# Experts in rounds of two chunks: both gates and ups, two down pieces, then both chunks' transposes

## The chip, the cores and the metric

The program runs on one NeuronCore of one Trainium2 chip. The metric is the device time of one execution in microseconds, lower is better. TensorE does the matrix products, VectorE and ScalarE the elementwise work and the reading of PSUM, GpSimd a few squares in the norms, and SyncE issues nearly all DMAs.

## The reference

A decoder trunk of two layers for 256 tokens of width 1024, float32. Layer 0 is a recurrent block and a dense SwiGLU, layer 1 is attention in a window and a mixture of eight experts. The change touches only the experts:

```python
logits = (h @ w_router)                       # 256 x 8
top_vals, top_idx = lax.top_k(logits, 2)
comb = one_hot(top_idx) weighted by softmax(top_vals)
for e in range(8):
    out += comb[:, e] * ((silu(h @ w_gate[e]) * (h @ w_up[e])) @ w_down[e])
```

`w_gate[e]` and `w_up[e]` are 1024 x 3584 and `w_down[e]` is 3584 x 1024.

## The kernel before

**Tiling.** An expert's 3584 hidden columns are cut into 14 chunks (`NCH`) of 256. A chunk has three pieces of weights of 1 MB each: gate, up and down. That makes 42 pieces (`PIECES`) per expert and 336 for eight. Each expert has room for 96 tokens (`CAP`); tokens beyond that would go to extra tiles in a loop behind the experts, which does not run with these inputs.

**Precision.** TensorE multiplies operands of the type fp32r, and each operand is split in two, a high part (the value cast, by ScalarE) and a low part (value minus high part, by VectorE). A product is three passes: high x high, low x high, high x low (`PASSES`). So a piece goes through four hands. SyncE loads it into one of 14 slots of a ring. ScalarE casts it into `w_hi` (line 656). VectorE subtracts it into `w_lo` (line 1237). TensorE uses both. `w_hi` and `w_lo` have room for three pieces (`PARTS`), so the cast of piece n waits until TensorE is through with piece n - 3 (`parts_used`). A slot of the ring is free again when its low part is done (`lo_done`), and SyncE's next load waits for that (lines 418 to 424).

**A chunk on TensorE.** `gate_up` (line 1807) makes gate and up of the chunk's 96 tokens, 24 matmuls of 256 columns each, in one PSUM bank, even and odd chunks in different banks. ScalarE applies silu (line 669), VectorE multiplies with up (line 1249). `turn_h` (line 1814) transposes the product in two transposes. ScalarE and VectorE evict it as high and low part (lines 673 and 1253, called `stage_ht`). `down` (line 1829) multiplies with the down piece, 12 matmuls of 512 columns, and adds up over all 14 chunks in two banks.

**Order.** Every engine runs a list written out by hand, without a planner. In `body`, for each chunk c from 2 to 13, TensorE does gate and up of c, down of c - 2, then the turn of c - 1. The down piece lags two chunks. `lead` starts the first expert with gate and up of chunks 0 and 1 and the turn of chunk 0. `cross` joins two experts: the next expert's chunks 0 and 1 stand between the last two downs of this one. `finish` ends the last expert. The tables `LEAD`, `BODY`, `CROSS` and `LAST` give the order of the pieces, which is the order of loads and of splits.

**Work strewn in.** Between the chunks stand these. `gather` picks the next expert's tokens with 32 matmuls (line 1795) and `stage_xg` evicts them. `weights_back` transposes the gate weights (line 1767) and ScalarE copies them (line 660). `stage_y` copies an expert's result out of PSUM, half by ScalarE (line 677) and half by VectorE (line 1258), once its last down is through. `scatter` multiplies it back to the tokens (line 1777) and `add_back` adds it to h on VectorE (line 1231). `next_onehots` makes the next expert's selection (lines 1262 and 1264). During expert 0 VectorE also builds the tables of overflow in pieces (`weights_of_choice`, `overflow_hits`, `overflow_tiles`, `overflow_columns`, `overflow_list`, lines 1173 to 1222). In the last expert's `finish`, `turn_back` transposes h in 16 transposes (line 1868) ahead of the last two downs.

## Time and profile before

| | |
|---|---|
| Three runs | 1494.76, 1498.63, 1498.02 us; median 1498.02 |
| The profiled execution's own time | 1499.07 us |
| Its span, first to last instruction | 1497.2 us |
| Mean granted clock of TensorE | 0.987 of full |
| Busy: TensorE matmuls, weight loads | 1459.7 us (97%), 1331.3 us (89%) |
| Busy: VectorE, ScalarE, GpSimd | 1161.0 us (78%), 919.4 us (61%), 42.7 us (3%) |
| DMA | 426.14 MB, mean 285 GB/s |
| The experts | from about 478 us to about 1482 us |

TensorE (PE) appears twice: PE are the matmuls and PEld the loads of the stationary operand, which overlap them. Matmuls are pipelined and the ends of their rows are modelled, so the distance from one start to the next says more than a duration. DVE is VectorE, ACT is ScalarE, SPq is the queue of DMAs that SyncE issues. A line number is that of the kernel shown above.

### The profile page before, as it was taken

What the parts mean: (1) busy time and instruction counts of PE and PEld (TensorE: products, weight loads), DVE (VectorE), ACT (ScalarE), POOL (GpSimd) and SP (SyncE); (2) the same over time, 40 slices, a digit from 0 to 9 for tenths busy, and PEclk for the clock granted to TensorE, in tenths of its full rate; (3) what the DMA queues carried; (4) which work ended last, traced back from release to release, by engine and by line L of the source; (5) the groups of instructions that cost most, each with busy time, mean ns of one, the idle gap of its engine ahead of it and who ended that gap; (6) DMA issues with size and microseconds to landing.
All of it is one profiled execution on the core that took longest, in us unless ns stands there. A gap on an engine that the chain in (4) does not pass through costs nothing.

```text
span 1497.2 us, 25391 instructions
## 1 busy us (share of the span) xinstructions
PE 1459.7 (97%) x10682; PEld 1331.3 (89%) x10682; DVE 1161.0 (78%) x1094; ACT 919.4 (61%) x904; POOL 42.7 (3%) x62
## 2 busy tenths in 40 slices
PE   8999999998899999999999999999999999999996
PEld 7889999998888999889889988988988898898894
DVE  6666555557545998898889888888888988888895
ACT  3744434343433776676767676676676766767675
POOL 2020000003001000000000000000000000000000
PEclk9999999999997999999999999999999999999999
DMA  8456555554206999999999899999989988999940
GB/s 325 141 205 211 184 182 197 175 192 141 85 29 279 383 381 351 359 355 342 342 353 383 333 350 352 346 340 362 360 319 363 375 334 340 366 342 341 362 174 30
DMA packets 60000, 426.14 MB, mean 285 GB/s; under 512 B 7024, under 2 KB 7152, under 8 KB 8688
## 3 DMA queue, kind: packets, MB, share of 16 engines
q1 hardware_dynamic: 58752, 422.60, 75.5%
q10 hardware_dynamic: 1136, 1.91, 0.4%
q8 instruction: 86, 1.41, 0.4%
q14 instruction: 26, 0.21, 0.0%
HBM read 423.44 MB, written 1.05 MB: 284 GB/s over the span
## 4 chain that ended last, share of the span: by engine, by line
PE 94%; DVE 3%; ACT 1%; POOL 1%; issue 1%; DMA 0%; DVEq 0%; ACTq 0%; SPq 0%; POOLq 0%
PE ps L1807 41%; PE ps L1829 21%; PE ps L1507 11%; PE ps L1529 5%; PE ps L1429 2%; PE ps L1795 2%; PE ps L1569 2%; PE ps L1777 2%; PE ps L1672 1%; PE ps L1814 1%; DVE w_lo L823 1%; PE ps L1461 1%; PE ps L1616 1%; PE ps L1444 1%; POOL hn L1387 1%
## 5 line engine op out<-in xcount | busy, mean ns | idle before, releaser
L1237 DVE TENSOR_TENSOR w_lo<-ring,w_hi 128x2048 fp32r<-128x2048 f32 x336 | 763.8, 2289 | 101.9 <-ACT w_hi L656 100.3
L656 ACT CAST w_hi<-ring 128x2048 fp32r<-128x2048 f32 x336 | 640.1, 1910 | 143.0 <-PE ps L1807 143.0
L1807 PE MATMUL ps<-w_hi,xg_hi 128*96 128x256 f32 x1792 | 249.3, 281 | 1.2 <-DVE xg_lo L1243 1.2
L1807 PE MATMUL ps<-w_lo,xg_hi 128*96 128x256 f32 x1792 | 242.1, 277 | 0.0
L1807 PE MATMUL ps<-w_hi,xg_lo 128*96 128x256 f32 x1792 | 241.6, 277 | 0.0
L1807 PEld LDWEIGHTS ps<-w_lo,xg_hi 128*96 128x96 f32 x1792 | 215.4, 161 | 1.2 <-DVE w_lo L1237 1.2
L1807 PEld LDWEIGHTS ps<-w_hi,xg_lo 128*96 128x96 f32 x1792 | 215.8, 161 | 0.0
L1807 PEld LDWEIGHTS ps<-w_hi,xg_hi 128*96 128x96 f32 x1792 | 213.6, 161 | 1.3 <-DVE xg_lo L1243 1.3
L823 DVE TENSOR_TENSOR w_lo<-ring,w_hi 128x2048 fp32r<-128x2048 f32 x56 | 129.8, 2320 | 80.9 <-ACT w_hi L471 80.9
L471 ACT CAST w_hi<-ring 128x2048 fp32r<-128x2048 f32 x56 | 106.5, 1903 | 112.1 <-PE ps L1507 94.1
L1829 PE MATMUL ps<-w_lo,ht_hi 128*96 128x512 f32 x448 | 123.4, 397 | 0.2 <-DVE w_lo L1237 0.2
L1829 PE MATMUL ps<-w_hi,ht_hi 128*96 128x512 f32 x448 | 122.9, 396 | 0.3 <-ACT w_hi L656 0.3
L1829 PE MATMUL ps<-w_hi,ht_lo 128*96 128x512 f32 x448 | 122.2, 394 | 0.0
L673 ACT CAST ht_hi<-ps 128x192 fp32r<-128x192 f32 x112 | 35.6, 318 | 117.9 <-PE ps L1814 117.7
L1829 PEld LDWEIGHTS ps<-w_lo,ht_hi 128*96 128x96 f32 x448 | 71.6, 161 | 33.6 <-DVE w_lo L1237 2.2
L1829 PEld LDWEIGHTS ps<-w_hi,ht_lo 128*96 128x96 f32 x448 | 72.2, 161 | 31.9
L1829 PEld LDWEIGHTS ps<-w_hi,ht_hi 128*96 128x96 f32 x448 | 67.1, 162 | 16.0 <-ACT w_hi L656 0.5
L1507 PE MATMUL ps<-u_hi,w_hi 128*128 128x256 f32 x448 | 58.1, 282 | 0.7 <-ACT u_hi L503 0.7
L1507 PE MATMUL ps<-u_hi,w_lo 128*128 128x256 f32 x448 | 57.3, 281 | 0.0
L1507 PE MATMUL ps<-u_lo,w_hi 128*128 128x256 f32 x448 | 57.3, 281 | 0.0
L1507 PEld LDWEIGHTS ps<-u_hi,w_hi 128*128 128x128 f32 x448 | 54.9, 189 | 1.6 <-ACT u_hi L503 1.1
L1253 DVE TENSOR_TENSOR ht_lo<-ps,ht_hi 128x192 fp32r<-128x192 f32 x112 | 38.9, 347 | 21.9 <-ACT ht_hi L673 21.9
(275 smaller groups left out, 1379.5 us busy)
## 6 DMA issues: line engine op xcount, KB each, us to landing
ring<-in_moe_w_gate SPq DMA_DIRECT2D x112, 1024.0 KB, 6.4
ring<-in_moe_w_up SPq DMA_DIRECT2D x112, 1024.0 KB, 6.2
ring<-in_moe_w_down SPq DMA_DIRECT2D x112, 1024.0 KB, 6.3
ring<-in_ffn_w_gate SPq DMA_DIRECT2D x14, 1024.0 KB, 4.8
ring<-in_ffn_w_up SPq DMA_DIRECT2D x14, 1024.0 KB, 4.8
ring<-in_ffn_w_down SPq DMA_DIRECT2D x14, 1024.0 KB, 4.8
ring<-in_lru_w_in SPq DMA_DIRECT2D x7, 1024.0 KB, 12.1
ring<-in_attn_w_qkv SPq DMA_DIRECT2D x6, 1024.0 KB, 4.8
```

What stands on the lines that cost most here:

```text
L471: nc.scalar.copy(w_hi[:, j % PARTS], ring[:, slot_at(j)]).then_inc(hi_done, 1)
L656: nc.scalar.copy(w_hi[:, (SPLITS + n) % PARTS], ring[:, s]).then_inc(hi_done, 1)
L673: nc.scalar.copy(ht_hi[:, c % 2], ps[:, 6 + c % 2, 0:2 * CAP].rearrange("p (f n) -> p f n", f=2)).then_inc(ht_hi_ready, 1)
L823: V.tensor_tensor(w_lo[:, j % PARTS], ring[:, slot_at(j)], w_hi[:, j % PARTS].bitcast(F32), ALU.subtract).then_inc(lo_done, 1)
L1237: V.tensor_tensor(w_lo[:, part], ring[:, ORDER_MOE[n % SLOTS]], w_hi[:, part].bitcast(F32), ALU.subtract).then_inc(lo_done, 1)
L1253: V.tensor_tensor(ht_lo[:, c % 2], ps[:, 6 + c % 2, 0:2 * CAP].rearrange("p (f n) -> p f n", f=2), ht_hi[:, c % 2].bitcast(F32), ALU.subtr ...
L1429: mm = nc.tensor.matmul(ps[:, p % 4, f * T:(f + 1) * T], col[:, k, f * P:(f + 1) * P], u_raw[:, k], start=(k == 0), stop=(k == KC - 1))
L1507: mm = nc.tensor.matmul(ps[:, 2 * (c % 2) + f, m * T:(m + 1) * T], w[b][:, k, f * P:(f + 1) * P], us[a][:, k], start=(k == 0 and (a, b) == ...
L1529: mm = nc.tensor.matmul(ps[:, 4 + d // 2, (d % 2) * T:(d % 2 + 1) * T], w[b][:, f, d * P:(d + 1) * P], fs[a][:, c % 2, f], start=False, st ...
L1569: mm = nc.tensor.matmul(ps[:, a % 2, b * T:(b + 1) * T], us[m][:, k, b * P:(b + 1) * P], w[n][:, k], start=False, stop=(k == KC - 1 and n ...
L1807: mm = nc.tensor.matmul(ps[0:CAP, c % 2, m * CHF:(m + 1) * CHF], xs[a][:, k], w[b][:, k], start=(k == 0 and (a, b) == (0, 0)), stop=(k == ...
L1829: mm = nc.tensor.matmul(ps[0:CAP, 2 + g, :], hs[a][:, c % 2, f], w[b][:, f, g * 512:(g + 1) * 512], start=(c == 0 and f == 0 and (a, b) == ...
```

## The change

The loop over chunks goes in steps of two. TensorE does gate and up of c and of c + 1, then the downs of c - 2 and c - 1, then the turns of c and c + 1. Loads, splits and evictions follow that order on SyncE, ScalarE and VectorE. `lead` turns chunk 1 as well, since the first body no longer does. In `cross` the two chunks of the next expert come first, then both last downs, then the transposes of the gate weights and the turns of the next expert's chunks 0 and 1. Scatters stand behind the turns of rounds c = 4 and 6, add-backs at the end of rounds 6 and 8, the copy of the gate weights behind `stage_y`. The numbers of instructions of each kind stay as they are.

```diff
         LEAD = [(m, c, 0) for c in range(2) for m in ("gate", "up")]
-        BODY = [(m, c - 2 * (m == "down"), 0) for c in range(2, NCH) for m in ("gate", "up", "down")]
-        CROSS = [("gate", 0, 1), ("up", 0, 1), ("down", NCH - 2, 0), ("gate", 1, 1), ("up", 1, 1), ("down", NCH - 1, 0)]
+        BODY = [(m, c, 0) for r in range(2, NCH, 2)
+                for m, c in (("gate", r), ("up", r), ("gate", r + 1), ("up", r + 1), ("down", r - 2), ("down", r - 1))]
+        CROSS = [("gate", 0, 1), ("up", 0, 1), ("gate", 1, 1), ("up", 1, 1), ("down", NCH - 2, 0), ("down", NCH - 1, 0)]
...
# ScalarE
             def body(i, y_at):
-                for c in range(2, NCH):
+                for c in range(2, NCH, 2):
                     n = BODY_AT + 3 * (c - 2)
+                    if c > 2 or y_at is not None:
+                        silu(i, c - 1, n - 3)
                     split(i, n)
+                    split(i, n + 1)
+                    if c == 2 and y_at is None:
+                        silu(i, 1, 3)
                     if c == 2 and y_at is not None:
                         stage_y(i, y_at)
-                    split(i, n + 1)
-                    silu(i, c - 1, n - 2 if c > 2 else y_at - 1 if y_at is not None else 3)
+                        weights_back(i - 1)
+                    split(i, n + 2)
                     stage_ht(i, c - 2)
-                    split(i, n + 2)
+                    stage_ht(i, c - 1)
+                    split(i, n + 3)
+                    silu(i, c, n + 1)
+                    split(i, n + 4)
+                    split(i, n + 5)
 
             def cross(i):
+                silu(i, NCH - 1, END_AT - 3)
+                stage_xg(i + 1)
                 split(i, END_AT)
-                act.wait_ge(parts_used, PIECES * i + (SPLITS + END_AT - 2 + 1))
-                stage_xg(i + 1)
                 split(i, END_AT + 1)
-                silu(i, NCH - 1, END_AT - 2)
+                split(i, END_AT + 2)
                 stage_ht(i, NCH - 2)
-                split(i, END_AT + 2)
+                stage_ht(i, NCH - 1)
                 split(i, END_AT + 3)
+                silu(i + 1, 0, END_AT + 1 - PIECES)
                 split(i, END_AT + 4)
-                weights_back(i)
-                silu(i + 1, 0, END_AT + 1 - PIECES)
+                split(i, END_AT + 5)
+
+            def finish(i, first=False):
+                silu(i, NCH - 1, END_AT - 3)
+                split(i, END_AT)
+                split(i, END_AT + 1)
+                stage_ht(i, NCH - 2)
                 stage_ht(i, NCH - 1)
...
# VectorE: body
-                for c in range(2, NCH):
+                for c in range(2, NCH, 2):
                     n = BODY_AT + 3 * (c - 2)
+                    if c > 2 or y_at is not None:
+                        gate_times_up(i, c - 1)
                     split(i, n)
+                    split(i, n + 1)
+                    if c == 2 and y_at is None:
+                        gate_times_up(i, 1)
                     if c == 2 and y_at is not None:
                         stage_y(i, y_at)
-                    split(i, n + 1)
-                    gate_times_up(i, c - 1)
+                    split(i, n + 2)
                     stage_ht(i, c - 2)
-                    split(i, n + 2)
-                    if first and c == 3:
+                    stage_ht(i, c - 1)
+                    split(i, n + 3)
+                    gate_times_up(i, c)
+                    split(i, n + 4)
+                    if first and c == 4:
                         weights_of_choice()
+                    if first and c == 6:
+                        overflow_tiles()
+                    if first and c == 8:
+                        overflow_columns(1)
+                    split(i, n + 5)
                     if first and c == 4:
                         overflow_hits()
-                    if first and c == 5:
-                        overflow_tiles()
-                    if first and c in (6, 7):
-                        overflow_columns(c - 6)
-                    if first and c == 9:
+                    if first and c == 6:
+                        overflow_columns(0)
+                    if first and c == 10:
                         overflow_list()
-                    if back and c in (4, 6):
-                        add_back(i - 1, c - 4)
-                        add_back(i - 1, c - 3)
+                    if back and c in (6, 8):
+                        add_back(i - 1, c - 6)
+                        add_back(i - 1, c - 5)
                     if c == 8:
                         next_onehots(i)
...
# TensorE
                 gate_up(i, 0, 0)
                 gate_up(i, 1, 2)
                 turn_h(i, 0)
+                turn_h(i, 1)
 
             def body(i, to_come, back=True, first=False):
-                for c in range(2, NCH):
+                for c in range(2, NCH, 2):
                     n = BODY_AT + 3 * (c - 2)
                     gate_up(i, c, n)
-                    down(i, c - 2, n + 2, first)
-                    if back and c in (3, 5):
-                        scatter(i - 1, c - 3)
-                        scatter(i - 1, c - 2)
-                    if c == 11 and to_come:
+                    gate_up(i, c + 1, n + 2)
+                    down(i, c - 2, n + 4, first)
+                    down(i, c - 1, n + 5)
+                    if c == 10 and to_come:
                         if back:
                             pe.wait_ge(added, 4 * i)
                         gather(i + 1)
-                    turn_h(i, c - 1)
+                    turn_h(i, c)
+                    turn_h(i, c + 1)
+                    if back and c in (4, 6):
+                        scatter(i - 1, c - 4)
+                        scatter(i - 1, c - 3)
 
             def cross(i):
                 pe.wait_ge(xg_ready, 2 * i + 4)
                 gate_up(i, 0, END_AT)
+                gate_up(i, 1, END_AT + 2)
+                down(i, NCH - 2, END_AT + 4)
+                down(i, NCH - 1, END_AT + 5)
                 weights_back(i)
-                down(i, NCH - 2, END_AT + 2)
-                turn_h(i, NCH - 1)
-                gate_up(i, 1, END_AT + 3)
-                down(i, NCH - 1, END_AT + 5)
                 turn_h(i + 1, 0)
+                turn_h(i + 1, 1)
...
             def finish(i, q, first=False):
-                turn_h(i, NCH - 1)
                 if first:
                     turn_back()
                 down(i, NCH - 2, END_AT)
```

## Rows read from the trace of the kernel before

**Rows 1.** The page's chain that ended last: shares of the span by engine.

```profile
PE 94%; DVE 3%; ACT 1%; POOL 1%; issue 1%; DMA 0%; DVEq 0%; ACTq 0%; SPq 0%; POOLq 0%
```

**Rows 2.** Groups by line, 480 to 1440 us: busy us, mean ns; idle before, releaser.

```profile
L1237 DVE TENSOR_TENSOR w_lo<-ring,w_hi 128x2048 fp32r<-128x2048 f32 x323 | 734.0, 2289 | 96.8 <-ACT w_hi L656 95.2
L656 ACT CAST w_hi<-ring 128x2048 fp32r<-128x2048 f32 x323 | 615.4, 1910 | 138.6 <-PE ps L1807 138.6
...
L1231 DVE TENSOR_TENSOR h<-ps,h 128x512 f32<-128x512 f32 x28 | 17.9, 683 | 0.0
```

**Rows 3.** Waits, 480 to 1440 us: who waited for whom, us, times, longest.

```profile
ACT w_hi L656 <- PE ps L1807: 138.6, 184, 1.1
...
PEld ps L1829 <- DVE w_lo L1237: 1.5, 7, 0.2
PEld ps L1807 <- DVE w_lo L1237: 1.2, 7, 0.2
...
SPq L424 <- DVE w_lo L1237: 548.6, 212, 6.0
```

**Rows 4.** Timeline of a steady chunk: start us, us, engine, line, operation, count.

```profile
711.61 0.33 PE L1814 MATMUL ps<-cst,hn 96*128 96x96 f32 x2
711.72 1.14 PE L1807 MATMUL ps<-w_hi,xg_hi 128*96 128x256 f32 x8
...
712.70 1.07 PE L1807 MATMUL ps<-w_hi,xg_lo 128*96 128x256 f32 x8
...
717.24 1.09 PE L1829 MATMUL ps<-w_hi,ht_hi 128*96 128x512 f32 x4
...
720.04 0.33 PE L1814 MATMUL ps<-cst,hn 96*128 96x96 f32 x2
```

**Rows 5.** Timeline behind an expert's border.

```profile
728.79 1.16 PE L1807 MATMUL ps<-w_hi,xg_hi 128*96 128x256 f32 x8
...
734.45 1.09 PE L1829 MATMUL ps<-w_hi,ht_hi 128*96 128x512 f32 x4
...
737.44 0.58 ACT L677 COPY hn<-ps 96x512 f32<-96x512 f32 x1 [3.63 <-PE ps L1829]
...
742.20 0.94 PEld L1807 LDWEIGHTS ps<-w_lo,xg_hi 128*96 128x96 f32 x8 [0.18 <-DVE w_lo L1237]
...
754.60 1.89 PE L1777 MATMUL ps<-gt_mem,hn 96*128 96x256 f32 x8
...
756.44 1.17 PE L1807 MATMUL ps<-w_hi,xg_hi 128*96 128x256 f32 x8
...
762.12 1.09 PE L1829 MATMUL ps<-w_hi,ht_hi 128*96 128x512 f32 x4
```

**Rows 6.** Timeline of the last transposes and the last two down pieces.

```profile
1472.88 0.49 PE L1814 MATMUL ps<-cst,hn 96*128 96x96 f32 x4
...
1473.22 1.91 PE L1868 MATMUL ps<-cst,h 128*128 128x128 f32 x16
...
1475.42 1.17 PE L1829 MATMUL ps<-w_hi,ht_hi 128*96 128x512 f32 x4 [0.30 <-ACT w_hi L656]
...
1476.44 1.10 PE L1829 MATMUL ps<-w_hi,ht_lo 128*96 128x512 f32 x4
...
1477.75 1.18 PE L1829 MATMUL ps<-w_lo,ht_hi 128*96 128x512 f32 x4 [0.21 <-DVE w_lo L1237]
```

**Rows 7.** Timeline at the end of expert 0's lead.

```profile
487.49 4.50 DVE L1237 TENSOR_TENSOR w_lo<-ring,w_hi 128x2048 fp32r<-128x2048 f32 x2 [0.86 <-ACT w_hi L656]
...
489.11 1.16 PE L1807 MATMUL ps<-w_hi,xg_hi 128*96 128x256 f32 x8
...
491.90 0.42 DVE L1249 TENSOR_TENSOR hn<-ps,hn 96x256 f32<-96x256 f32 x1
```

**Rows 8.** Timeline of TensorE in the attention.

```profile
406.55 0.63 PE L1595 MATMUL ps<-cst,ring 128*128 128x128 f32 x4 [3.09 <-DVE ring L1075]
```

**Rows 9.** Windows: busy us of each engine, PEclk, DMA share, GB/s.

```profile
408.00:411.30 3.30, 3.30 (x10) 2.44 (x10) 1.45 (x3) 1.50 (x8) 0.00 (x0) 0.50 0.57 241
```

More of the change, by code:

```diff
@@ L696, in body @@
             def body(i, y_at):
-                for c in range(2, NCH):
+                for c in range(2, NCH, 2):
                     n = BODY_AT + 3 * (c - 2)
+                    if c > 2 or y_at is not None:
+                        silu(i, c - 1, n - 3)
                     split(i, n)
+                    split(i, n + 1)
+                    if c == 2 and y_at is None:
+                        silu(i, 1, 3)
                     if c == 2 and y_at is not None:
                         stage_y(i, y_at)
-                    split(i, n + 1)
-                    silu(i, c - 1, n - 2 if c > 2 else y_at - 1 if y_at is not None else 3)
+                        weights_back(i - 1)
+                    split(i, n + 2)
                     stage_ht(i, c - 2)
-                    split(i, n + 2)
+                    stage_ht(i, c - 1)
[3 more added lines that the diff above has]
+                    split(i, n + 5)
             def cross(i):
+                silu(i, NCH - 1, END_AT - 3)
+                stage_xg(i + 1)
                 split(i, END_AT)
-                act.wait_ge(parts_used, PIECES * i + (SPLITS + END_AT - 2 + 1))
-                stage_xg(i + 1)
                 split(i, END_AT + 1)
-                silu(i, NCH - 1, END_AT - 2)
+                split(i, END_AT + 2)
                 stage_ht(i, NCH - 2)
-                split(i, END_AT + 2)
+                stage_ht(i, NCH - 1)
                 split(i, END_AT + 3)
+                silu(i + 1, 0, END_AT + 1 - PIECES)
                 split(i, END_AT + 4)
-                weights_back(i)
-                silu(i + 1, 0, END_AT + 1 - PIECES)
-                stage_ht(i, NCH - 1)
                 split(i, END_AT + 5)
             def finish(i, first=False):
-                silu(i, NCH - 1, END_AT - 2)
+                silu(i, NCH - 1, END_AT - 3)
+                split(i, END_AT)
+                split(i, END_AT + 1)
                 stage_ht(i, NCH - 2)
-                split(i, END_AT)
                 stage_ht(i, NCH - 1)
-                split(i, END_AT + 1)
                 if first:
@@ L1311, in cross @@
             def cross(i):
+                gate_times_up(i, NCH - 1)
+                stage_xg(i + 1)
                 split(i, END_AT)
-                stage_xg(i + 1)
                 split(i, END_AT + 1)
-                gate_times_up(i, NCH - 1)
+                split(i, END_AT + 2)
                 stage_ht(i, NCH - 2)
-                split(i, END_AT + 2)
+                stage_ht(i, NCH - 1)
                 split(i, END_AT + 3)
+                gate_times_up(i + 1, 0)
                 split(i, END_AT + 4)
-                gate_times_up(i + 1, 0)
-                stage_ht(i, NCH - 1)
                 split(i, END_AT + 5)
@@ L1325, in finish @@
                 gate_times_up(i, NCH - 1)
+                split(i, END_AT)
+                split(i, END_AT + 1)
                 stage_ht(i, NCH - 2)
-                split(i, END_AT)
                 stage_ht(i, NCH - 1)
-                split(i, END_AT + 1)
                 if first:
```

## The prediction

> **What bounds the kernel now.** I read the chain of waits first: 94% of the span is TensorE's own work [rows 1], so only what sits on TensorE's path counts. Then the groups by line for the expert stage (480 to 1440 us): the low-part subtraction takes 734.0 us of VectorE and the cast 615.4 us of ScalarE out of 960 [rows 2]; both have slack. The waits agree: TensorE's weight loads waited 1.5 and 1.2 us in all for a low part, while ScalarE waited 138.6 us for TensorE [rows 3]. The queue of loads, SP, waits for VectorE to free slots, 548.6 us for one of its two lines [rows 3], so transfers are early, not late. Last I read the order of time. A steady chunk runs from turn to turn in 720.04 - 711.61 = 8.43 us: 0.11 until the gate starts, 5.52 for gate and up (711.72 to 717.24), 2.80 for down [rows 4]. With 112 chunks that is 944 us of the span of 1497.2, and the change reorders nothing else.
>
> **The same work at two paces.** A gate or up pass of 8 matmuls takes 0.91 us in the steady chunk (712.70 to 717.24 is five of them), or 0.114 a matmul. In other chunks gate and up take 5.66 (728.79 to 734.45) or 5.68 (756.44 to 762.12) in place of 5.51 or 5.52 [rows 4, 5], with the granted clock at full speed and nobody waited for: 0.117 a matmul. Going through all starts of that kind I count 37 slow chunks of 112: the whole lead of expert 0 and its next two, then in each later expert three (in two experts two) after the transposes that bring the gates back, and one after each pair of scatters (14 of 14; the scatter at 754.60 is such a place [rows 5]). They cost 37 x 0.165 = 6.1 us now. A slow pace lasts through an unbroken run of gate and up (96 matmuls in the lead) and changes only across a down and a turn.
>
> **The change part by part.** All against the profiled execution's 1499.07 us (span 1497.2 and 1.9 around it).
>
> 1. *Turns in pairs.* Number and size of matmuls, casts, subtractions and loads stay. There are 111 places where TensorE goes from other work into transposes and back (the last two turns stand together already); they become 56. A place with two transposes costs 0.11 to the gate's start and 0.07 in the gate's first pass (0.98 against 0.91 later): 0.18 [rows 4]. A place with four exists once, at the end: 1472.88 to the next kind of work at 1473.22, 0.34, to which the same 0.07 may come [rows 6]. So merging two places is worth between 2 x 0.18 - 0.41 = -0.05 and 2 x 0.18 - 0.34 = +0.02; from the idle of the weight loads alone, which the matmul rows don't confirm, I would get at most 0.17. I take +0.02: 55 x 0.02 = **-1.2 us**, ends +2.8 and -9.
>
> 2. *Expert 0's lead now turns chunk 1 too.* That turn waits for chunk 1's product, and nothing stands between them on TensorE any more. Before, chunk 2's gate started at 489.11, right behind turn 0, and the product, queued on VectorE behind two subtractions (4.50 us from 487.49), ran from 491.90 for 0.41 [rows 7]. VectorE's order there stays the same (two splits, then the product). So turn 1 can start at about 492.4 and chunk 2's gate at 492.5 in place of 489.11: **+3.4 us**, between 3.2 and 3.6. Behind that wait stand gate 2 and all that follows. VectorE and ScalarE catch up meanwhile, but TensorE waited for neither afterwards, so nothing is given back.
>
> 3. *That idle and the clock.* TensorE idled 3.09 us before 406.55 and ran at 0.50 of its clock from 408.0 to 411.3 [rows 8, 9]; 0.50 is the 1.2 GHz level. The new idle is as long. If it does the same, half of 3.3 us is lost, 1.6; with an even chance **+0.8 us**, ends 0 and 1.6. The Trainium skill, "TensorE: Matmul & The Clock Gate", section "Why this matters for your kernels", asks for no idle over some 3 us between bursts of matmuls, else the clock falls to half. By that rule the fall is certain here and the sum is 0.8 higher; the trace's one comparable gap agrees with it.
>
> 4. *Steady round.* Take the first gate's start as 0: gate 0, up 2.8, gate 5.5, up 8.25, downs 10.95 and 13.75, turns 16.55, next round 16.83. A cast starts 0.25 behind the piece three before its own and takes 1.91; a subtraction follows and takes 2.2 to 2.3 [rows 2]. The first down's high part is cast from 6.15 to 8.05 (behind silu, which waits for up) and its low part done by 10.3; they are needed at 10.95 and 12.8. The second is done at 10.4 and 12.7, needed at 13.75 and 15.6. The second chunk's silu runs from 11.2 and its product ends at 13.1, needed at 16.6. The two evictions of turned h sit in 1.9 to 2.5 on ScalarE, ahead of a cast that can't start before 3.05. Nothing is late: **0**. The tightest round is the one of c = 8, where two add-backs (0.683 each [rows 2]) and the next one-hots (about 1.0) now stand together on VectorE: the next low part is done at 17.8, needed at 18.65. Expert 0's table work, two helpers a round of 1.1 to 1.5 each, leaves about as much. If that cover of 0.85 were gone, each expert would pay what is missing, 8 x 0.3 or so.
>
> 5. *The expert's border.* Before, ScalarE met the eviction of y between the splits of chunk 2's gate and up and stood 3.63 us for the last down, so a low part came late and TensorE stood 0.18 at 742.20 [rows 5]; gate and up took 0.2 more than the chunks beside it, in each of 7 experts. Now both casts come first. **-1.4 us**; by the weight loads' waits it could be 2.7 [rows 3]. Staging the next tokens now lies beside two downs. It was hidden beside one before: 0.
>
> 6. *The end.* The last split stood behind the eviction of turn 12, so TensorE came 0.45 late from the 16 transposes (1473.22 plus 16 x 0.11 against 1475.42) and 0.38 late between passes (1477.75 - 1476.44 = 1.31 against 0.93), with some 0.15 of refilling [rows 6]. Now both casts come ahead of it, and the low part of h is ready about when the transposes end: **-1.0 us**, ends 0 and -1.2.
>
> 7. *Loads.* The same 336 loads in the order in which the splits take them, 14 slots deep. SP is moved past no other wait. With 11 pieces (31 us) between issue and use there is nothing to pay; if a load were late the ScalarE cast would show it, and none does now: **0**.
>
> 8. *Pace.* A slow pace can now change only once per two chunks. If after each cause it lasts as many turn places as before, a scatter costs two slow chunks for one, and the return of the gates three or so: about 7 slow of 14 per expert in place of 5, 53 in all. 16 x 0.165 = **+2.6 us**, ends -6.1 (none slow) and 75 x 0.165 = +12.4 (all slow).
>
> Sum: 1499.07 - 1.2 + 3.4 + 0.8 - 1.4 - 1.0 + 2.6 = 1502.3. The profiled execution lies 1.05 above the median of the three runs, 1498.02; against it the forecast is 1501.2, and I say 1501.
>
> **Rivals.**
>
> *The slow pace becomes the rule (slower).* One mechanism: the pace of gate and up is fixed by how TensorE leaves the turn in front. For it: the fourth transpose in the row at the end starts at the weight loads' own spacing, as the two behind a scatter do, and those were followed by the slow pace every time. Against it: two turns behind a down led to the fast pace in every steady chunk. It decides at the first gate pass of a round; from 0.93 us a pass in most rounds on, the loss outweighs all gains. Time: 1502.3 - 2.6 + 12.4 = 1512.1, by the median 1511.
>
> *The slow pace goes (faster).* Four transposes might always leave it fast. Then 1502.3 - 2.6 - 6.1 = 1493.6, by the median 1492.5; without the fall of the clock 1491.7. For it: fast is where the chain of chunks now ends up when left alone. Against it: scatters and the gates' return now lead straight or with fewer turns into the gates.
>
> *Turns in pairs are worth the full 0.17.* The weight loads' rows speak for it, the matmul starts against. 55 x 0.15 more gives 1494, by the median 1493.
>
> *VectorE is the bound in the crowded rounds (slower).* If c = 8 and expert 0 run out of cover I expect 2 to 4 us: 1504 to 1505.
>
> **Chances.** Forecast as summed 0.46; slow pace throughout 0.28; slow pace gone 0.12; full worth of pairs 0.06; VectorE late 0.08. What a measurement can tell from no change is 0.3%, 4.5 us: 1493.5 to 1502.5. Of the forecast's cases some 0.33 fall inside and 0.13 above, the VectorE case and the slow pace above, the other two mostly below: faster 0.17, same 0.38, slower 0.45. Range 1493 to 1512; the likeliest case alone has 1497 to 1505.
>
> **What would show it.** Right: turns in rows of four; one idle of about 3.3 us of TensorE near 489 behind the product, perhaps with a stretch at 0.50 clock behind it; no wait of weight loads for low parts near the eviction of y; a round of 16.8 us when fast and 17.2 when slow; no gaps around the last transposes. Wrong: rounds under 16.7, which would mean that the turns cost less than I read; a wait of casts for loads; TensorE waiting for a low part in rounds 8 to 10; or the pace of gate and up the same in all rounds, which decides between the rivals.

## The result, and the profile of the changed kernel

| kernel | median, us | lowest to highest | runs |
|---|---|---|---|
| before | 1496.81 | 1494.76 to 1498.63 | 7 |
| changed | 1505.61 | 1496.79 to 1506.65 | 7 |

The ratio of changed to before is 1.0046, with an interval of 1.0026 to 1.0066. That is 6.9 us more (3.9 to 9.9); the two medians lie 8.8 apart. Both are above the 0.3% that can be told from no change: slower. The forecast was 1501 in a range of 1493 to 1512.

The profiled execution of the changed kernel took 1496.79 us (span 1494.9), less than the 1499.07 of the profiled one before. This is the one number that misleads. In the changed kernel's trace the first gather of the experts starts at 459.16, in the trace of before at 469.66, and the code up to there is the same in both. The dense feed-forward shows where part of that comes from. First after, then before, in the timeline of TensorE (start us, us, engine, line, operation, count):

```profile
203.95 1.98 PE L1525 MATMUL ps<-u_lo,w_hi 128*128 128x256 f32 x16
205.76 1.98 PE L1525 MATMUL ps<-u_hi,w_lo 128*128 128x256 f32 x16
```

```profile
206.17 2.05 PE L1507 MATMUL ps<-u_hi,w_lo 128*128 128x256 f32 x16
208.05 1.22 PE L1507 MATMUL ps<-u_hi,w_hi 128*128 128x256 f32 x9
```

A pass of 16 takes 1.81 us in one execution (113 ns a matmul) and 1.88 in the other (118 ns), at full clock in both. The stage's code is the same in all twelve kernels of this study, and of their twelve profiled executions two (this one and e8's) had the quick pace; I take this for much of the spread between runs of one kernel, which was not traced run by run. Another part is the clock: behind an idle of 2.85 us of TensorE, which begins at 75.07 before and at 74.50 after, the trace of before has 0.50 from 76.8 to 83.6, and that of after has 1.00 there, which saves it 2.35 us on the same matmuls. So the two traces are compared from the first gather on only. From there to the transposes back at the end it is 1003.56 us before and 1012.63 after, **+9.08**; from there to the last matmul 12.63 and 11.68, **-0.95**. The net, +8.1, lies inside the interval of the runs.

What bounds the kernel has not changed; the chain of waits of after:

```profile
PE 92%; DVE 3%; ACT 2%; issue 1%; POOL 1%; DMA 0%; DVEq 0%; ACTq 0%; SPq 0%; POOLq 0%
```

**The lead of expert 0** answers to [rows 7]. Timeline of after, TensorE and VectorE (TensorE's matmuls are a turn, a turn, then gate passes of chunk 2):

```profile
476.71 4.50 DVE L1245 TENSOR_TENSOR w_lo<-ring,w_hi 128x2048 fp32r<-128x2048 f32 x2 [0.86 <-ACT w_hi L657]
...
478.22 0.33 PE L1832 MATMUL ps<-cst,hn 96*128 96x96 f32 x2
...
481.12 0.42 DVE L1257 TENSOR_TENSOR hn<-ps,hn 96x256 f32<-96x256 f32 x1
...
481.59 0.38 PE L1832 MATMUL ps<-cst,hn 96*128 96x96 f32 x2 [3.04 <-DVE hn L1257]
481.75 1.69 PE L1825 MATMUL ps<-w_hi,xg_hi 128*96 128x256 f32 x8
483.24 1.91 PE L1825 MATMUL ps<-w_hi,xg_lo 128*96 128x256 f32 x8
484.95 1.37 PE L1825 MATMUL ps<-w_lo,xg_hi 128*96 128x256 f32 x8
```

Before, the gate of chunk 2 came 0.11 behind the turn; now 481.75 - 478.22 = 3.53, so 3.4 us are lost to the product on VectorE. Behind the idle the first two passes take 1.49 and 1.71 in place of 0.93. The windows (us, then busy time of each engine, PEclk, DMA share, GB/s) show the granted clock:

```profile
465.10:482.10 17.00, 12.79 (x109) 12.45 (x109) 13.53 (x13) 15.04 (x14) 0.00 (x0) 1.00 1.01 421
482.10:485.50 3.40, 3.40 (x18) 3.40 (x17) 2.17 (x3) 0.23 (x1) 0.00 (x0) 0.50 1.01 419
```

0.50, the 1.2 GHz level, for 3.4 us: fifteen matmuls started 213 ns apart in place of 117, which is 1.44 us.

**Rounds.** The timeline of TensorE from expert 1's gather (L1813), over the border into that expert, to its first scatter (L1795) and the gates behind it answers to [rows 4] and [rows 5]. L1832 is a turn, L1825 gate and up, L1847 down, L1785 the transposes of the gate weights:

```profile
568.61 3.71 PE L1813 MATMUL ps<-sel_mem,work 128*128 128x96 f32 x32
...
572.15 0.49 PE L1832 MATMUL ps<-cst,hn 96*128 96x96 f32 x4
572.43 1.13 PE L1825 MATMUL ps<-w_hi,xg_hi 128*96 128x256 f32 x8
...
583.37 1.09 PE L1847 MATMUL ps<-w_hi,ht_hi 128*96 128x512 f32 x4
...
588.96 0.49 PE L1832 MATMUL ps<-cst,hn 96*128 96x96 f32 x4
...
605.77 0.38 PE L1785 MATMUL ps<-cst,sel_mem 128*96 128x128 f32 x2
605.99 0.50 PE L1832 MATMUL ps<-cst,hn 96*128 96x96 f32 x4
606.27 1.17 PE L1825 MATMUL ps<-w_hi,xg_hi 128*96 128x256 f32 x8
...
617.54 1.09 PE L1847 MATMUL ps<-w_hi,ht_hi 128*96 128x512 f32 x4
...
623.13 0.49 PE L1832 MATMUL ps<-cst,hn 96*128 96x96 f32 x4
...
640.24 0.49 PE L1832 MATMUL ps<-cst,hn 96*128 96x96 f32 x4
640.57 1.92 PE L1795 MATMUL ps<-gt_mem,hn 96*128 96x256 f32 x8
642.14 1.30 PE L1825 MATMUL ps<-w_hi,xg_hi 128*96 128x256 f32 x8
...
653.55 1.09 PE L1847 MATMUL ps<-w_hi,ht_hi 128*96 128x512 f32 x4
```

Four turns in a row, as the change says. The round behind the gather takes 588.96 - 572.15 = 16.81 us, with 10.94 for its 96 gate and up matmuls (572.43 to 583.37). The two transposes at 605.77 bring the next gate weights back; behind them the same 96 take 11.27 (606.27 to 617.54), and the rounds behind that 17.14 and 17.11, at full clock. From each gather to the next it repeats: two stretches of 96 at the fast pace, then five at the slow one, scatter or none. Ahead of the first such gather all six are slow, and behind the last gather six of eight. That makes 42 of 56 stretches slow, or 84 chunks of 112, where before had 37.

Among the waits of the expert stage (for whom, us, times, longest) there is no wait of a weight load for a low part any more, as the 14 of [rows 3] were:

```profile
PEld ps L1832 <- DVE hn L1257: 3.2, 1, 3.2
```

**The end** answers to [rows 6]:

```profile
1471.79 1.91 PE L1890 MATMUL ps<-cst,h 128*128 128x128 f32 x16
1473.57 1.14 PE L1847 MATMUL ps<-w_hi,ht_hi 128*96 128x512 f32 x4
1474.55 1.09 PE L1847 MATMUL ps<-w_hi,ht_lo 128*96 128x512 f32 x4
1475.47 1.09 PE L1847 MATMUL ps<-w_lo,ht_hi 128*96 128x512 f32 x4
```

The down starts 1.78 behind the sixteen transposes (2.20 before), and its passes follow 0.98 and 0.92 apart (1.02 and 1.31 before).

### The profile page after: what moved, and what is told of

The parts are those of the page before. It is cut to its first block, busy times and chain, and to the rows that moved or that the text cites. A ratio compares the mean times of both kernels' runs of the same rounds, so it can differ in the third digit from the quotient of the medians.

```text
span 1494.9 us, 25384 instructions
## 1 busy us (share of the span) xinstructions
PE 1454.6 (97%) x10682; PEld 1329.6 (89%) x10682; DVE 1162.4 (78%) x1094; ACT 921.3 (62%) x904; POOL 42.7 (3%) x62
## 4 chain that ended last, share of the span: by engine, by line
PE 92%; DVE 3%; ACT 2%; issue 1%; POOL 1%; DMA 0%; DVEq 0%; ACTq 0%; SPq 0%; POOLq 0%
PE ps L1825 41%; PE ps L1847 21%; PE ps L1525 10%; PE ps L1547 5%; PE ps L1447 2%; PE ps L1813 2%; PE ps L1587 2%; PE ps L1795 2%; PE ps L1690 1%; PE ps L1832 1%; DVE w_lo L831 1%; PE ps L1634 1%; ACT w_hi L472 1%; PE ps L1462 1%; POOL hn L1405 1%
## 5 line engine op out<-in xcount | busy, mean ns | idle before, releaser
L1825 PE MATMUL ps<-w_hi,xg_hi 128*96 128x256 f32 x1792 | 250.0, 281 | 1.2 <-DVE xg_lo L1251 1.2
L1825 PE MATMUL ps<-w_hi,xg_lo 128*96 128x256 f32 x1792 | 244.9, 279 | 0.0
L1825 PE MATMUL ps<-w_lo,xg_hi 128*96 128x256 f32 x1792 | 244.2, 278 | 0.0
L1825 PEld LDWEIGHTS ps<-w_hi,xg_hi 128*96 128x96 f32 x1792 | 218.0, 162 | 2.4 <-DVE xg_lo L1251 1.3
L1825 PEld LDWEIGHTS ps<-w_hi,xg_lo 128*96 128x96 f32 x1792 | 218.9, 162 | 0.0
L1825 PEld LDWEIGHTS ps<-w_lo,xg_hi 128*96 128x96 f32 x1792 | 218.2, 162 | 0.0
L1847 PE MATMUL ps<-w_hi,ht_lo 128*96 128x512 f32 x448 | 123.0, 396 | 0.0
L1847 PE MATMUL ps<-w_lo,ht_hi 128*96 128x512 f32 x448 | 122.2, 394 | 0.0
L1847 PE MATMUL ps<-w_hi,ht_hi 128*96 128x512 f32 x448 | 121.8, 394 | 0.0
L1847 PEld LDWEIGHTS ps<-w_hi,ht_lo 128*96 128x96 f32 x448 | 72.1, 161 | 32.4
L1847 PEld LDWEIGHTS ps<-w_lo,ht_hi 128*96 128x96 f32 x448 | 72.1, 161 | 32.3
L670 ACT ACTIVATE hn<-ps 96x256 f32<-96x256 f32 x112 | 42.7, 382 | 89.1 <-PE ps L1825 89.1
L1847 PEld LDWEIGHTS ps<-w_hi,ht_hi 128*96 128x96 f32 x448 | 69.6, 161 | 23.1
L1525 PEld LDWEIGHTS ps<-u_lo,w_hi 128*128 128x128 f32 x448 | 53.0, 188 | 0.0
```

The lines of the kernel that those rows point to most:

```text
L670: nc.scalar.activation(h_tok[:, c % 2], ps[0:CAP, c % 2, 0:CHF], ACT.Silu).then_inc(m_silu, 1)
L1525: mm = nc.tensor.matmul(ps[:, 2 * (c % 2) + f, m * T:(m + 1) * T], w[b][:, k, f * P:(f + 1) * P], us[a][:, k], start=(k == 0 and (a, b) == ...
L1825: mm = nc.tensor.matmul(ps[0:CAP, c % 2, m * CHF:(m + 1) * CHF], xs[a][:, k], w[b][:, k], start=(k == 0 and (a, b) == (0, 0)), stop=(k == ...
L1847: mm = nc.tensor.matmul(ps[0:CAP, 2 + g, :], hs[a][:, c % 2, f], w[b][:, f, g * 512:(g + 1) * 512], start=(c == 0 and f == 0 and (a, b) == ...
```

## The experiments

The disputed term is the slow pace. My theory at the outset was that the pace of a stretch of gate and up depends on how TensorE leaves the block in front, with no one waited for, and that longer rounds leave fewer places at which it can change back. The rivals were a fixed cost of the pairs of turns, the alternation of work itself, and the scatters. In the tables, *stage* is what the profiled execution took from the first gather to the last matmul against the kernel before (1003.56 + 12.63 = 1016.19), worked out from the starts in its trace. Up to 1 us of a stage is not the change's: from the first gather to the first gate, in code that is the same everywhere, the twelve traces took between 7.18 and 8.22. *Slow* counts chunks of an expert's 14, as the later experts have it. Each ratio is to runs of the kernel before that were taken beside it, so ratios compare better than medians.

| kernel | median, us (runs) | ratio to before, interval | stage, us | slow |
|---|---|---|---|---|
| changed | 1505.61 (7) | 1.0046 (1.0026 to 1.0066) | +8.1 | 10 of 14 |
| e1_lead | 1501.59 (6) | 1.0031 (1.0019 to 1.0044) | +3.6 | 10 of 14 |
| e2_before_fixed | 1495.05 (11) | 0.9980 (0.9970 to 0.9990) | -2.7 | 4 of 14 |
| e4_pairs | 1509.01 (5) | 1.0075 (1.0061 to 1.0088) | +9.5 | 7 of 14 |
| p1_probe | 1509.12 (1) | none | +11.3 | varied |
| e5_b_at_gather | 1497.04 (11) | 0.9987 (0.9972 to 1.0002) | -1.8 | 6 of 14 |
| e6_rounds_b_late_s | 1492.12 (5) | 0.9963 (0.9949 to 0.9977) | -8.3 | 0 of 14 |
| e7_turns_apart | 1498.79 (10) | 1.0006 (0.9996 to 1.0015) | +1.9 | 10 of 14 |
| e8_rounds_b_moved | 1487.97 (8) | 0.9960 (0.9941 to 0.9980) | -8.5 | 0 of 14 |
| e9_one_zero | 1488.42 (11) | 0.9949 (0.9934 to 0.9965) | -8.3 | 0 of 14 |
| e10_late_s | 1500.77 (10) | 1.0032 (1.0017 to 1.0047) | +3.5 | 10 of 14 |

### e1_lead: the lead's second turn back behind the next gate and up

```
# TensorE's program; on ScalarE and VectorE one split now stands ahead of turn 1's eviction
 gate_up(i, 1, 2)
 turn_h(i, 0)
-turn_h(i, 1)
 # body, c == 2 of expert 0 only
 gate_up(i, c, n)
+turn_h(i, 1)
 gate_up(i, c + 1, n + 2)
```

> The changed kernel, with expert 0's turn of chunk 1 moved from the lead to behind gate and up of chunk 2, so that TensorE doesn't stand for the product. Theory (the lead's wait costs 3.4 us and makes the clock fall for another 1.4): the stretch from the first gather to the second shrinks by about 4.9 us of 109.5, no stretch at 0.5 clock behind 482 us, and the time goes from 1505.6 to about 1501. Rival (the wait is only moved, or the clock falls anyway): 1504 to 1506, with the idle or the slow clock elsewhere in expert 0. The paces of the later experts should stay as in the changed kernel: 10 slow chunks of 14.

Measured: 1501.59. The trace has neither the idle nor a clock of 0.50 in expert 0. The second turn, now between two runs of gate and up, in its TensorE timeline:

```profile
492.73 0.33 PE L1838 MATMUL ps<-cst,hn 96*128 96x96 f32 x2
492.85 1.17 PE L1831 MATMUL ps<-w_hi,xg_hi 128*96 128x256 f32 x8
```

The gate starts 0.12 behind the turn again. From gather to gather expert 0 takes 104.95 us in place of 109.45. Of that the gather up to the first gate, which the edit doesn't touch, is 8.19 against 7.75; from the first gate on it is 96.76 in place of 101.70. Experts 1 to 6 stay at 126.53 with the same pattern. So 4.9 us of the loss belong to the lead: the forecast's wait, 3.42, and the 1.44 of the clock. The rest is elsewhere.

### e2_before_fixed: the border and the end alone, on the kernel before

```
 split(i, n)
 if c == 2 and y_at is not None:
+    silu(i, 1, y_at - 1)        # ScalarE; on VectorE gate_times_up(i, 1)
+    split(i, n + 1)
     stage_y(i, y_at)
-split(i, n + 1)
-silu(i, c - 1, ...)
...
 # finish: the split of the last but one down piece ahead of both turned chunks
+split(i, END_AT)
 stage_ht(i, NCH - 2)
-split(i, END_AT)
 stage_ht(i, NCH - 1)
```

> The kernel before with only the changed order at the experts' border (the product and the split of chunk 2's up ahead of the eviction of y) and at the end (split ahead of the eviction of the last two turned chunks). Theory (these two are the change's only real gains, 0.2 us for each of 7 borders and 0.9 at the end): 2.3 us faster than before, and if the wait at the border is what keeps the pace slow for a chunk more, up to 1 us on top: 1494 to 1495 against 1497. Rival (the gains come only with the rounds of two): within 0.5 us of before.

Measured: 1495.05, 2.5 below before. The period of an expert falls from 126.11 to 125.76, the last one with the end by 0.9, and the weight loads' waits of [rows 3] are gone. These two parts of the change gain what they were meant to, without rounds.

### e4_pairs: turns in pairs, but gate and up alternating with down

```
 gate_up(i, c, n)
-gate_up(i, c + 1, n + 2)
-down(i, c - 2, n + 4, first)
+down(i, c - 2, n + 2, first)
+gate_up(i, c + 1, n + 3)
 down(i, c - 1, n + 5)
 turn_h(i, c)
 turn_h(i, c + 1)
```

> Turns in pairs alone: gate, up and down alternate as before (48 matmuls of gate and up, then 12 of down), but the two turns of a round stand together behind the second down. Theory A (a turn place changes a slow pace to fast with some chance, and half as many places give half the chances): slow rounds about as in the changed kernel, 8 to 10 slow chunks of 14, time about that of the changed kernel, 1503 to 1507. Theory B (the unbroken run of 96 gate and up matmuls or of 24 downs holds the slow pace, not the turns): the pace falls back to fast as in the kernel before, 5 slow chunks of 14, time about 1500. Theory C (four transposes in a row leave the slow pace slow): all rounds behind a disturbance slow until the gather, as in the changed kernel, but the pace may change at the down in the middle of a round.

Measured: 1509.01, a ratio of 1.0075 against the changed kernel's 1.0046; the two intervals just overlap, and the stages differ by 1.3 us. Its waits in the expert stage hold a cost that none of the theories had:

```profile
PE ps L1826 <- DVE hn L1254: 6.3, 10, 1.1
```

The turn of chunk c + 1 stands one down behind its up. That is too soon for the product in three rounds of expert 0 (the lead waits as in the changed kernel, for less) and, in each later expert, in the round of c = 8, where VectorE also has the add-backs and the next one-hots. And the pace changes where there is no turn at all. TensorE from the border on:

```profile
740.82 0.56 PE L1819 MATMUL ps<-w_hi,xg_hi 128*96 128x256 f32 x3
...
746.31 1.09 PE L1841 MATMUL ps<-w_hi,ht_hi 128*96 128x512 f32 x4
...
749.11 1.11 PE L1819 MATMUL ps<-w_hi,xg_hi 128*96 128x256 f32 x8
...
754.72 1.09 PE L1841 MATMUL ps<-w_hi,ht_hi 128*96 128x512 f32 x4
```

48 matmuls take 5.49 here behind four turns (740.82 to 746.31) and 5.61 straight behind a down (749.11 to 754.72); in other rounds it is the other way round. Of the 55 rounds of this kernel 54 have one slow stretch of 48 and one fast one, so the down between the two goes with a change of pace nearly every time, which none of the theories expected. The theory survives in its wide form (the block in front decides) and fails in its narrow one (the turn decides). As a test of pairs alone it is spoilt by the new wait.

### p1_probe: another piece between downs and gates in each expert

```
 v = i if back else 0
 down(i, c - 2, n + 4, first)
+if v == 1: turn_h(i, c)                      # a turn between the two downs
 down(i, c - 1, n + 5)
+if v == 2 and c in (4, 6): scatter(...) x2   # scatters ahead of the turns
 turn_h(i, c); turn_h(i, c + 1)
+if v in (3, 4): one zero matmul of 128 or 256 columns
+if v in (5, 6): one or two more transposes of h_tok
```

> The changed kernel with another piece of work between the downs and the gates in each expert's rounds, to see what sets the pace of gate and up. Expert 1: turn of c between the two downs, turn of c + 1 behind them. Expert 2: scatters ahead of the turns. Experts 3 and 4: one extra matmul of a row of zeros (128 and 256 columns) behind the turns. Experts 5 and 6: one and two extra transposes of h into a bank not in use, whose results nobody reads. Expert 7 and 0 as changed. Theory A (only the number of places counts): expert 1 gets back to fast within a round or two, 3 to 6 like 7. Theory C (four transposes in a row keep it slow): expert 1 fast after one round, 5 and 6 slow. Theory D (what counts is the phase in which TensorE leaves the block, to a few ns): some of 3 to 6 are fast in all rounds and others slow in all, each the same in every round of its expert.

One run, 1509.12. With a turn between the downs expert 1 changes pace in both directions (period 126.11). Scatters ahead of the turns leave expert 2 slow. In experts 5 and 6, with one and two extra transposes ahead of the gates, two of six and three of six stretches are fast. In experts 3 and 4 a zero matmul stands in front of twelve stretches of 96: ten are fast, and the one over the border is slow in both. TensorE in expert 3:

```profile
868.40 0.50 PE L1832 MATMUL ps<-cst,hn 96*128 96x96 f32 x4
...
885.55 0.49 PE L1832 MATMUL ps<-cst,hn 96*128 96x96 f32 x4
885.97 0.22 PE L1884 MATMUL ps<-zero_mem 1*128 1x128 bf16 x1
886.13 1.08 PE L1825 MATMUL ps<-w_hi,xg_hi 128*96 128x256 f32 x7
...
897.13 1.09 PE L1847 MATMUL ps<-w_hi,ht_hi 128*96 128x512 f32 x4
```

The piece costs what it gains, though: gates start 0.58 behind the turns (885.55 to 886.13) in place of 0.28, and the round takes 885.55 - 868.40 = 17.15, as a slow one does. One small instruction in front of 96 equal ones goes with another pace of all of them, which speaks for "how the block in front ends" as against a count of turns. The block alone doesn't settle it, though. At the borders into experts 4 and 5 the transposes of the gate weights and four turns, the block behind which the changed kernel is slow each time, stand behind a slow stretch and are followed by a fast one.

### e5_b_at_gather: on e2, the gate weights' transposes ahead of the gather

In the changed kernel the stretches behind the gather are fast, and those behind the border's transposes slow, in every expert. So I moved the transposes there, first in the order of the kernel before. (The expectation says this of all traces so far; e4's and the probe's hold exceptions, as the borders just named.)

```
 # cross: gate_up(i, 0, END_AT)
-weights_back(i)
 # body, c == 11
+weights_back(i, 7)      # into another bank; ScalarE copies it at c == 12
 gather(i + 1)
 turn_h(i, c - 1)
...
 # body, c == 12
+pe.wait_ge(g_ready, i + 1)
 turn_h(i, c - 1)
```

> The kernel before with the border and the end as in e2_before_fixed, and the transposes of the gate weights moved from the middle of the border to just ahead of the gather of the next tokens. In all traces so far the chunks behind a gather ran fast, and the chunks behind the gate weights' transposes slow. Theory (the pace is set by what stands in front of the gates): the two slow chunks at the border go away, 2 slow chunks of 14 are left (one behind each pair of scatters) or 3, the period from gather to gather falls from 125.76 to about 125.3, and the time from 1495.05 to 1492 (7 x 2 x 0.165 = 2.3 us, and some 0.1 a border for the places merged). Rival (the slow pace at the border comes from the border itself, its evictions or the new operand): no change of the slow chunks, 1495.

Measured: 1497.04, a miss: 6 slow chunks of 14, period 126.09 against e2's 125.76. The gather doesn't reset the pace:

```profile
572.05 0.38 PE L1774 MATMUL ps<-cst,sel_mem 128*96 128x128 f32 x2
572.27 3.71 PE L1802 MATMUL ps<-sel_mem,work 128*128 128x96 f32 x32
575.82 0.33 PE L1821 MATMUL ps<-cst,hn 96*128 96x96 f32 x2
575.93 1.15 PE L1814 MATMUL ps<-w_hi,xg_hi 128*96 128x256 f32 x8
...
581.59 1.09 PE L1836 MATMUL ps<-w_hi,ht_hi 128*96 128x512 f32 x4
```

5.66 for 48, slow, behind transposes, gather and *two* turns; ahead of the move this place was fast.

### e6, e8 and e10: the same move in the changed kernel, and the scatters

All three stand on e1. e6 moves the transposes as above and the scatters, with their add-backs, one round (two chunks) later; e8 moves the transposes alone; e10 the scatters alone.

```
 # e6 and e8: in cross
-weights_back(i)
 # e6 and e8: in body, c == 10; ScalarE's copy moves to its c == 12
+weights_back(i, 7)
 gather(i + 1)
 turn_h(i, c)
+pe.wait_ge(g_ready, i + 1)
 turn_h(i, c + 1)
 # e6 and e10
-if back and c in (4, 6): scatter(...) x2
+if back and c in (6, 8): scatter(...) x2
```

> The changed kernel with expert 0's lead as in e1_lead, the transposes of the gate weights just ahead of the gather, and the scatters a round later (behind c = 6 and 8, add-backs in rounds 8 and 10), so that the disturbances stand as late as they can before the gather. Theory (rounds of two don't get out of the slow pace by themselves; the gather does it): fast from the gather until the first scatter, so 4 slow chunks of 14 in place of 10; period 126.53 - 6 x 0.165 = 125.5; time from 1501.6 to 1494.5. With that, slow rounds are what made the changed kernel slower. Rival (rounds of two are slow for another reason, such as the long run of gates): 9 or 10 slow chunks again, 1501.

> e6_rounds_b_late_s with the scatters back behind c = 4 and 6, so that against e1_lead only the transposes of the gate weights have moved, from the border to just ahead of the gather. Theory (the slow pace enters a round only behind those transposes at the border, and rounds of two pass on the pace they find, through scatters too): no slow chunk in experts 1 to 7, period 124.9, time 1492. Rival (the late scatters did it): the first scatter, behind c = 4, brings the slow pace as before, 6 slow chunks of 14, period 125.9, time 1498.

> e1_lead with only the scatters moved, behind c = 6 and 8; the gate weights' transposes stay at the border. Theory: slow from the border to the gather as in e1_lead, 10 slow chunks of 14, period 126.5, time 1501.6. Rival (the late scatters did it): 4 to 6 slow chunks, 1495 to 1498.

Measured: e6 1492.12 with no slow chunk in experts 1 to 7, better than forecast; e8 1487.97 and as clean; e10 1500.77 with e1's pattern and period unchanged. Here is e8's TensorE, at the places that answer to those of the changed kernel:

```profile
563.60 0.38 PE L1792 MATMUL ps<-cst,sel_mem 128*96 128x128 f32 x2
563.82 3.71 PE L1820 MATMUL ps<-sel_mem,work 128*128 128x96 f32 x32
567.37 0.49 PE L1839 MATMUL ps<-cst,hn 96*128 96x96 f32 x4
...
601.27 0.46 PE L1832 MATMUL ps<-w_hi,xg_hi 128*96 128x256 f32 x2
...
612.22 1.09 PE L1854 MATMUL ps<-w_hi,ht_hi 128*96 128x512 f32 x4
...
634.95 1.92 PE L1802 MATMUL ps<-gt_mem,hn 96*128 96x256 f32 x8
636.52 1.27 PE L1832 MATMUL ps<-w_hi,xg_hi 128*96 128x256 f32 x8
...
647.60 1.09 PE L1854 MATMUL ps<-w_hi,ht_hi 128*96 128x512 f32 x4
```

The stretch of c = 2 (601.27 to 612.22) takes 10.95 in place of 11.27, and the one behind a scatter 11.08 in place of the changed kernel's 11.41. The scatter never made the pace slow here; it passed on the one it found. (Not so with fewer turns: in e7 below, with two ahead of a scatter in place of four, the stretch behind an expert's second pair of scatters is fast, 11.08, though the one ahead is slow, 11.39.) The period falls from 126.53 to 124.93, and the table's stage is 12.2 us under e1's by one piece of TensorE's work moved. This version beats both kernels: its median is 8.1 us under that of before, and by the ratio it is 6.0 us faster (3.0 to 8.8). Its profiled execution also drew the quick dense pace, so its span isn't compared, its stage is.

### e7_turns_apart: a turn between the two downs in every round but the border's

```
 down(i, c - 2, n + 4, first)
+turn_h(i, c)
 down(i, c - 1, n + 5)
-turn_h(i, c)
 turn_h(i, c + 1)
```

> e1_lead with the pairs of turns undone, and the rounds kept: the turn of c stands between the two downs, that of c + 1 behind them. Theory (twice as many places to get out of the slow pace): as in expert 1 of the probe, period 126.1 to 126.2, with 7 to 8 slow chunks of 14; time 1498.5 to 1499.5. Rival (the pairs of turns have no part in it): slow chunks and time as e1_lead, 1501.6, or above it by what the merged places were worth, 55 x 0.05 = 2.8 us.

Measured: 1498.79, with a ratio of 1.0006, but the period is 126.58, above the 126.1 expected. Between the first two gathers two of seven stretches are slow (period 125.62), between all later ones five. Without the rows of four turns the later experts have as many slow chunks as in e1, so these rows are not the cause of the slow pace. And one and the same sequence can run in either pace.

### e9_one_zero: e6 with one zero matmul behind expert 0's second round

```
 turn_h(i, c + 1)
+if first and c == 2: one zero matmul of 128 columns
```

> e6_rounds_b_late_s with one matmul of zeros behind the first round of expert 0, where five rounds ran slow; in the probe such a matmul was followed by the fast pace in 10 of 10 rounds, at a cost of 0.3 us in the round. Theory (rounds of two pass on the pace): all rounds of expert 0 from c = 4 fast, 5 x 0.33 - 0.3 = 1.3 us less in the first period (104.71 to 103.4), time 1490.8. Rival (expert 0 is slow for a reason of its own, such as its table work on VectorE): no change of the pace, 1492.4.

Measured: 1488.42, within the spread of e6 and e8, and a miss for the theory: the stretch behind the zero matmul is slow here, and expert 0 takes 104.69 as in e6 (104.71). What went with the fast pace ten times of twelve in the probe is no switch.

## Why the prediction was right or wrong

The sign and the place of the change's costs were right, and one size was far off: the pace, by 5.2 us. Step 1 was off by 1.0 the other way and step 3 by 0.6. The forecast's sum gives +3.2 against the profiled execution of before, the traces give +8.1. That 1505.61 still lies in the range is owed to the width of the range, which reached up to the rival's time.

- *Step 1, turns in pairs* (-1.2). A fast round takes 16.81 against 2 x 8.43 in [rows 4]: 0.04 to 0.05 a pair, about -2.2 in 55. That is more than either value of step 1 (-0.05 and +0.02): a place with four turns costs 0.28 to the gate's start, not the 0.34 read at the end. The weight loads' 0.17 was not there. (The -1.2 written for 55 x 0.02 should be -1.1.)
- *Step 2, the lead* (+3.4): 3.42 from the first gate's start to chunk 2's (14.83 after, 11.41 before). Shown by taking it away in e1.
- *Step 3, the clock* (+0.8, an even chance of 1.6): in the profiled execution the clock fell, and it cost 1.44. The even chance was a fair one. The attention's idle of 3.08 to 3.10 us [rows 8], in code that is the same in all twelve kernels, was followed by a clock of 0.50 in seven of the twelve traces and by 1.00 in five. The second kind, in e1 (timeline of TensorE, then the window):

```profile
404.67 0.63 PE L1619 MATMUL ps<-cst,ring 128*128 128x128 f32 x4 [3.09 <-DVE ring L1086]
```

```profile
404.00:412.00 8.00, 7.33 (x56) 6.96 (x57) 4.66 (x11) 4.46 (x19) 0.00 (x0) 1.00 0.40 132
```

The lead's own idle was followed by 0.50 in both traces that have it (3.04 in after, 3.05 in the probe); how many other runs of the changed kernel paid for it is not known. The prediction called the gap in the attention the one comparable gap; the trace of before has another, 2.85 us from 75.07 with 0.50 behind it, and that idle was followed by 0.50 in eight of the twelve. The Trainium skill, "TensorE: Matmul & The Clock Gate", section "Why this matters for your kernels", wants no idle over some 3 us between bursts of matmuls. The trace of after agrees, with 3.04 us of idle and 3.4 us at 0.50. The five traces at 1.00 behind 3.09 us and the eight at 0.50 behind 2.85 do not, and the measurement decides.
- *Step 4, the steady round* (0): nothing late, in the rounds c = 8 and 10 either. The rival of a late VectorE is out.
- *Step 5, the border* (-1.4): the waits are gone. e2, without rounds, gains 0.35 an expert, of which one slow chunk fewer is 0.165; the 0.19 left is the forecast's 0.2, seven times.
- *Step 6, the end* (-1.0): -0.95.
- *Step 7, loads* (0): no cast waits for a load in either.
- *Step 8, the pace* (+2.6): **this term was mis-sized.** 84 slow chunks, not 53; 47 more than before at 0.165 make +7.8.

3.42 + 1.44 + 7.8 - 1.4 - 2.2 = 9.1, against 9.08 in the traces; with the end 8.1. That is closer than the terms deserve: from the first gather to the first gate, where the change does nothing, the trace of after took 7.75 and that of before 8.04, so some 0.3 us is left without a term.

What failed in step 8 is the sentence "if after each cause it lasts as many turn places as before". I counted places per cause. The slow pace enters at one place an expert, behind the gate weights' transposes, and in rounds of four turns nothing leads out of it until the gather, where two turns behind a down had led out of it within three chunks. The rival "the slow pace becomes the rule" named this outcome and its own point of decision (0.93 us a pass in most rounds), and by that point it came true, in 42 of 56 stretches, so the time lies between the forecast's and its 1511. Its reason was half right. The pace changes only at a block between stretches, never inside one, but four turns alone leave it fast (572.15), and the same block is followed by either pace in different traces. The scatters, which I held guilty of two slow chunks each, were innocent in this order: e10 moved them and nothing changed, e8 left them and the stretches behind them were fast.

Shown: the lead and the clock (e1); border and end (e2); that in this order the place of two transposes, with their bank and their eviction, decides ten chunks of 14 (e8 against e1 and e10). It does so whatever pace expert 0 had begun with: the lead's 96 matmuls were slow in after and e1 and fast in e10, all with ten slow chunks, and fast in e6 and e8 and slow in e9, all with none. Not shown: what in the machine fixes the pace. The order of instructions alone doesn't: up to chunk 3 of expert 0 the code of e1, e6, e8, e9 and e10 is the same, and the lead, chunk 2 and chunk 3 ran slow, fast, slow in e1; fast, fast, slow in e6 and e8; slow, slow, fast in e9; and fast, slow, slow in e10. e5 and e8 move the same transposes to the same place and get opposite results; e7's expert 1 and its others run the same order at different paces, and the probe's zero matmul failed in e9. The rounds of expert 0 from c = 4 to its gather stayed slow in every kernel of this order. I can say which sequences gave which pace here, not predict it for a new one.

## What to carry to other kernels

When one instruction type fills the span, divide its time by its count in every stretch before the forecast; a 3% difference at full clock, with nobody waited for, is a term of the sum and can be the largest. Reordering around such a run should be judged by the count of slow stretches in the new trace, and it is worth trying each short interloper (transposes of weights, a scatter) in another place, alone. And a turn that waits for another engine's work on the matmuls just ahead of it needs other matmuls in between, in the lead too: 3.0 us of idle cost 4.9 with the clock.

## What the runs showed of the hardware

- Matmuls of 256 columns with a weight load each ran at two paces, 113.3 and 116.7 ns start to start with 96-column weights, and 113.3 and 117.8 with 128, both at full granted clock; each stretch of 48 or 96 kept one pace from end to end. The Trainium skill, "TensorE: Matmul & The Clock Gate", section "Wait — 56ns, not 53.3ns?", gives the start to start of back-to-back matmuls at the full clock as columns over 2.4 GHz plus some 2.5 ns. An estimate from it for 256 columns is 109.2 ns. No run here shows that value, and the section names one pace, not two; the measurement decides.
- In the dense stage an execution held one pace throughout (1.81 or 1.88 us a pass), quick in two of twelve traces of the same code. Single runs of such a kernel are no measure of a change under 1%: e8's went from 1480.31 to 1493.15.
- Behind an idle of TensorE of 3.08 to 3.10 us the granted clock went to 0.50 in seven of twelve traces and stayed at 1.00 in five; behind 2.85 to 2.86 us it went to 0.50 in eight and stayed in four.
- The first 96 gate and up matmuls of expert 0, the same code in all twelve kernels, took 11.28 to 11.30 us in seven traces and 10.98 to 11.01 in five. From expert 1 to expert 6, the order of slow and fast stretches was the same in every expert in eight of the twelve traces, and the periods agreed to 0.03 us.
- Behind a single bf16 matmul on one row, 96 matmuls ran at the quick pace ten times in twelve in the probe, and not in e9.
